# Hybrid attention and HGRN2 block: keys and inputs of three row tiles turned on VectorE and ScalarE instead of TensorE

## What is computed

```python
def hgrn2_chunkwise(q, f_logit, i, lb):
    f = lb[None, None] + (1.0 - lb[None, None]) * jax.nn.sigmoid(f_logit.astype(f32))
    kk = 1.0 - f
    ...
    G = jnp.cumsum(log_f.reshape(B, nc, CHUNK, HGRN_HEADS, HGRN_HEAD_K), axis=2)
    q_dec = qf * jnp.exp(G)
    k_dec = kf * jnp.exp(-G)
    A = jnp.einsum('bclhk,bcmhk->bchlm', q_dec, k_dec)
    A = jnp.where(causal[None, None, None], A, 0.0)
    o_intra = jnp.einsum('bchlm,bcmhv->bclhv', A, vf)
    U = jnp.einsum('bclhk,bclhv->bchkv', k_to_end, vf)
    ...
    o_inter = jnp.einsum('bclhk,bchkv->bclhv', q_dec, S_prev)
```

## Time and profile before

| | us |
|---|---|
| median of 3 executions (890.5 to 892.84) | 891.44 |
| the profiled execution | 892.7 |
| its span, first to last instruction | 890.9 |
| PE busy (4730 matmuls) | 879.2 |
| DVE busy | 524.4 |
| ACT busy | 422.5 |
| POOL busy | 113.9 |

### The profile page before, as it was taken

How to read it: one execution, slowest core, us unless ns; L and a number is a source line. 1 busy time by engine, 2 the same in 40 slices (tenths; PEclk the granted TensorE clock), 3 DMA queues, 4 the chain that set the end, 5 groups by cost and what they waited for, 6 DMA issues and landing times.

```text
span 890.9 us, 12324 instructions
## 1 busy us (share of the span) xinstructions
PE 879.2 (99%) x4730; PEld 721.8 (81%) x4730; DVE 524.4 (59%) x848; ACT 422.5 (47%) x736; POOL 113.9 (13%) x90
## 2 busy tenths in 40 slices
PE   7999999999999999999999999999999999999997
PEld 6887788888888778888888877888888877788886
DVE  6778867864656765665153686465524367655523
ACT  7666456664544444545144534454523453445322
POOL 0000013420200001421020000142111000013012
PEclk9999999999999999999999999999999999999999
DMA  8686766629958543552785654345378544443463
GB/s 313 209 308 221 252 219 226 222 93 376 417 198 303 200 169 132 176 179 98 289 325 197 225 190 142 142 142 194 134 263 330 189 149 158 164 142 144 145 248 127
DMA packets 52922, 186.03 MB, mean 209 GB/s; under 512 B 5888, under 2 KB 6144, under 8 KB 52864
## 3 DMA queue, kind: packets, MB, share of 16 engines
q1 hardware_dynamic: 50128, 178.29, 56.1%
q10 hardware_dynamic: 2736, 6.95, 2.0%
HBM read 141.18 MB, written 44.04 MB: 208 GB/s over the span
## 4 chain that ended last, share of the span: by engine, by line
PE 98%; DMA 1%; issue 0%; DVE 0%; ACT 0%; SPq 0%; DVEq 0%
PE bank L452 65%; PE bank L461 10%; PE score_b L461 5%; PE turn_b L461 5%; PE score_b L481 2%; PE bank L532 2%; PE turn_b L503 2%; PE turn_b L549 2%; PE bank L540 2%; PE turn_b L552 2%; PE score_b L525 1%; PE turn_b L495 1%; DMA x_in<-in_x 1%; PE score_b L559 0%; PE score_b L560 0%; PE turn_b L445 0%
## 5 line engine op out<-in xcount | busy, mean ns | idle before, releaser
L452 PE MATMUL bank<-h_hi,w_hi 128*128 128x512 f32 x832 | 327.4, 395 | 1.6 <-ACT h_hi L728 1.6
L452 PE MATMUL bank<-h_hi,w_lo 128*128 128x512 f32 x832 | 328.0, 394 | 0.0
L452 PE MATMUL bank<-h_lo,w_hi 128*128 128x512 f32 x832 | 325.9, 392 | 0.0
L452 PEld LDWEIGHTS bank<-h_lo,w_hi 128*128 128x128 f32 x832 | 156.5, 188 | 35.1 <-issue 3.3
L452 PEld LDWEIGHTS bank<-h_hi,w_hi 128*128 128x128 f32 x832 | 156.7, 188 | 34.5 <-ACT h_hi L728 1.8
L452 PEld LDWEIGHTS bank<-h_hi,w_lo 128*128 128x128 f32 x832 | 156.7, 188 | 33.7 <-issue 1.0
L1220 POOL TENSOR_TENSOR mix_lo<-v_r,mix_hi 128x512 fp32r<-128x512 f32 x16 | 21.1, 1317 | 544.6 <-ACT v_r L839 544.6
L908 DVE TENSOR_TENSOR w_lo<-w_raw,w_hi 128x1024 fp32r<-128x1024 f32 x37 | 44.9, 1221 | 32.4 <-ACT w_hi L691 32.4
L812 ACT ACTIVATE kv_tok<-score_b 128x1024 f32<-128x1024 f32 x16 | 16.4, 1025 | 83.5 <-PE score_b L525 83.5
L461 PE MATMUL bank<-w_hi,mix_lo 128*128 128x512 f32 x128 | 50.5, 395 | 0.0
L691 ACT ACTIVATE w_hi<-w_raw 128x1024 fp32r<-128x1024 f32 x38 | 39.7, 1051 | 22.1 <-issue 9.3
(11 more groups left out here) (169 smaller groups left out, 1393.8 us busy)
## 6 DMA issues: line engine op xcount, KB each, us to landing
w_hi<-kept_hi SPq DMA_DIRECT2D x96, 512.0 KB, 3.8
w_lo<-kept_lo SPq DMA_DIRECT2D x96, 512.0 KB, 4.7
w_raw<-in_weights SPq DMA_DIRECT2D x38, 512.0 KB, 5.4
kept_hi<-w_hi SPq DMA_DIRECT2D x34, 512.0 KB, 6.0
kept_lo<-w_lo SPq DMA_DIRECT2D x34, 512.0 KB, 7.2
x_in<-in_x_rows SPq DMA_DIRECT2D x8, 1024.0 KB, 7.4
x_in<-in_x SPq DMA_DIRECT2D x15, 512.0 KB, 6.6
out<-q_gate ACTq DMA_DIRECT2D x9, 512.0 KB, 9.0
```

Of the source, the lines that this page charges most:

```text
L452: mm = pe.matmul(acc(w)[:, :], stationary[:, s, k, :], moving[:, k, :], start=(m == 0), stop=(m == 3 * KT - 1), skip_group_check=True)
```

## The change

For tiles 1 to 3 (`DVE_TURN = 1`) PE no longer turns keys and inputs.

- Keys: DVE turns `k_mid` into `kv_tok` by 16 transposes, each of a square of 32 partitions by 32 columns in all four row blocks at once (`turn_keys`, 32x4x32). For heads 1 to 3 they follow the head's `v_r` and `to_next`; for head 0 they stand at the end of that step, behind the softmax of the attention.
- Inputs: DVE turns the 32 by 32 squares of `v_r` in place into `f_d` by one 128x512 transpose. ACT carries the squares to their partitions by 16 copies of 32x4x32 (`place_values`), at the end of its part of the step, behind the two squares of the output of the head before.
- Inputs of heads 1 and 3 go to the upper half of `probs` (`v_spare`), of heads 0 and 2 to `kv_tok` as before.
- `head_sum`, which writes `score_b`, gets the waits on the softmax and on the head before that stood ahead of the transposes. Two waits of PE on `kv_ready` for the use of `score_b` go.

```diff
+DVE_TURN = 1
...
+        def v_tok(t, h):
+            return v_spare if t >= DVE_TURN and h % 2 else kv_tok[:, 1, :]
...
+            def turn_head(t, h):
+
                 pe.wait_ge(m_sub.sem, m_sub.after(t, PAIRS - 1 if gate(h) >= SCORES0 + CHUNKS else (gate(h) - SCORES0) // 2))
                 pe.wait_ge(o_rstd.sem, o_rstd.after(t, h - 2))
                 for a, src in enumerate((k_mid, v_r)):
...
+            def head_scores(t, h):
+
+                pe.wait_ge(k_mid_done.sem, k_mid_done.after(t, h))
+                pe.wait_ge(tile_read.sem, tile_read.after(t, value(h)))
+                if t < DVE_TURN:
+                    turn_head(t, h)
...
                 pe.wait_ge(kv_ready.sem, kv_ready.after(t, h))
+                if t >= DVE_TURN:
+                    pe.wait_ge(k_blocks, blocks_done(t, h))
                 pe.wait_ge(a_masked.sem, a_masked.after(t, h))
...
                 pe.wait_ge(o_low.sem, o_low.after(t, h))
+                if t >= DVE_TURN:
+                    pe.wait_ge(m_sub.sem, m_sub.after(t, PAIRS - 1))
+                    pe.wait_ge(o_rstd.sem, o_rstd.after(t, h - 1))
...
+            def place_values(t, h):
+                act.wait_ge(v_blocks, blocks_done(t, h))
+                act.wait_ge(o_done.sem, o_done.after(t, h - 2))
+                for i in range(4):
+                    for j in range(4):
+                        copy = act.activation(square(v_tok(t, h), j, i), square(f_d[:, :], i, j), ACT.Copy)
+                copy.then_inc(kv_ready.sem, 1)
...
-                        if s == gate(head):
+                        if s == gate(head) and t < DVE_TURN:
                             act.wait_ge(kv_turned.sem, kv_turned.after(t, head))
...
                         if s == out_step(head):
+                            if t >= DVE_TURN and head < HEADS - 1:
+                                act.wait_ge(v_blocks, blocks_done(t, head + 1))
                             act.wait_ge(o_done.sem, o_done.after(t, head))
...
+                    for head in range(HEADS):
+                        if s == gate(head) and t >= DVE_TURN:
+                            place_values(t, head)
...
+            def turn_keys(t, h):
+
+                dve.wait_ge(k_mid_done.sem, k_mid_done.after(t, h))
+                dve.wait_ge(u_done.sem, u_done.after(t, h - 1))
+                for i in range(4):
+                    for j in range(4):
+                        last = dve.transpose(square(kv_tok[:, 0, :], j, i), square(k_mid[:, :], i, j))
+                last.then_inc(k_blocks, 1)
...
+                        if t >= DVE_TURN:
+                            dve.wait_ge(tile_read.sem, tile_read.after(t, value(h_of)))
+                            dve.transpose(f_d[:, :], v_r[:, :]).then_inc(v_blocks, 1)
                         then(t, dve.tensor_tensor(to_next[:, :], to_end[:, h_of % 2, 0:PAIRS - 1], to_mid[:, h_of % 2, 1:], ALU.mult))
+                        if t >= DVE_TURN and h_of:
+                            turn_keys(t, h_of)
...
+                    if s == gate(0) and t >= DVE_TURN:
+                        turn_keys(t, 0)
```

More of the change, by code:

```diff
@@ L180, in hybrid_block @@
         kv_tok = sb("kv_tok", [2, N])
+        v_spare = probs[:, PAIRS:, :].rearrange("p q n -> p (q n)")
         a_t = sb("a_t", [N])
@@ L277, in hybrid_block @@
         y_scaled, finished_pool = count("y_scaled", 2), count("finished_pool", 2)
+        k_blocks, v_blocks = sem("k_blocks"), sem("v_blocks")
         pool_setup = sem("pool_setup")
@@ L312, in wait_split, with blocks_done, square @@
                 engine.wait_ge(w_ready[slot], 32 * uses(slot, FRESH, i + 1))
+        def v_tok(t, h):
+            return v_spare if t >= DVE_TURN and h % 2 else kv_tok[:, 1, :]
+        def blocks_done(t, h):
+            return (t - DVE_TURN) * HEADS + h + 1
+        def square(ap, i, j):
+            return by_pair(ap)[32 * i:32 * i + 32, :, 32 * j:32 * j + 32]
         def state_pairs(t):
@@ L474, in scores @@
                 for h in range(HEADS):
-                    if gate(h) + 1 == SCORES0 + 2 * q:
+                    if gate(h) + 1 == SCORES0 + 2 * q and t < DVE_TURN:
                         pe.wait_ge(kv_ready.sem, kv_ready.after(t, h))
@@ L513, in turn_values @@
                 mm.then_inc(values_turned.sem, 1)
-            def head_scores(t, h):
-                pe.wait_ge(k_mid_done.sem, k_mid_done.after(t, h))
-                pe.wait_ge(tile_read.sem, tile_read.after(t, value(h)))
+            def turn_head(t, h):
                 pe.wait_ge(m_sub.sem, m_sub.after(t, PAIRS - 1 if gate(h) >= SCORES0 + CHUNKS else (gate(h) - SCORES0) // 2))
@@ L537, in head_states @@
                 pe.wait_ge(kv_ready.sem, kv_ready.after(t, h))
+                if t >= DVE_TURN:
+                    pe.wait_ge(k_blocks, blocks_done(t, h))
                 pe.wait_ge(a_masked.sem, a_masked.after(t, h))
                 for p in range(state_pairs(t)):
-                    mm = pe.matmul(head_b[:, pair(p)], kv_tok[:, 0, pair(p)], kv_tok[:, 1, pair(p)], start=True, stop=True)
+                    mm = pe.matmul(head_b[:, pair(p)], kv_tok[:, 0, pair(p)], v_tok(t, h)[:, pair(p)], start=True, stop=True)
                 mm.then_inc(u_done.sem, 1)
@@ L548, in head_out @@
                     empty = t == 0 and p == 0
-                    mm = pe.matmul(out_b[:, pair(p)], kv_tok[:, 1, pair(p)], a_t[:, pair(p)],
+                    mm = pe.matmul(out_b[:, pair(p)], v_tok(t, h)[:, pair(p)], a_t[:, pair(p)],
                                    start=True, stop=empty, skip_group_check=True)
@@ L630, in _ @@
                 pe.wait_ge(mixa_lo.sem, mixa_lo.after(t, QT - 1))
-                pe.wait_ge(kv_ready.sem, kv_ready.after(t, HEADS - 1))
+                if t < DVE_TURN:
+                    pe.wait_ge(kv_ready.sem, kv_ready.after(t, HEADS - 1))
                 order = [(2 * w + i, b) for w in range(3) for b in range(4) for i in range(2)] + [(KT - 2, b) for b in range(4)]
```

## The result

| | before | after |
|---|---|---|
| median, us | 892.14 (4 executions) | 882.98 (4 executions) |
| span of the profiled execution | 890.9 | 882.8 |
| DVE busy | 524.4 | 587.1 |
| ACT busy | 422.5 | 467.5 |

The ratio is 0.9896, interval 0.9884 to 0.9908: 9 us faster. The forecast was 883.6 within 881.8 to 892.0. For the profiled execution it was 884.9, which took 884.64 (892.7 before), 8.1 us less. The medians lie 9.2 apart, partly because a fourth execution of the kernel before moved its median from 891.44, on which the forecast stood, to 892.14.

The account below looks back on a forecast made before the run. PE was taken as the bound, busy 879.2 of 890.9 us. Saving 8.8 us less 1.0 of new waits gave -7.8, 892.7 to 884.9 for the profiled execution; the median, 1.3 lower, was forecast at 883.6, range 881.8 to 892.0.

Parts of the forecast that it names:

- PE's saving: Transposes leaving PE in tiles 1 to 3: 0.74 us saved a head, twelve heads, 8.8 us in all.
- ACT's copies: ACT's 16 copies of turned inputs a head: 0.29 us each from start to start, up to 0.31 allowed, 4.6 us.
- The rope rows: Profile rows of four ACT rope copies of 32x512, 2.40 us together, from which the 0.29 us copy price was taken.
- Rival 1: No new wait: ACT's small copies overlap like full ones (0.19 us), or a chain has more room; 882.6 us, chance 0.22.
- DVE's squares: DVE's 16 transposes of keys a head: 0.30 us each, 4.8 us in all.
- Rivals 2 and 3: Rival 2, and a dearer case: DVE squares at 0.48 us make the mask the bound, 895.3 us, chance 0.16.
- The new wait: PE waits at `A` for head 3's `v_r` in tiles 1 and 2: 0.4 to 0.8 us each, taken as 1.0 together.
- The sum: Whole profiled execution: -8.8 us saved plus 1.0 of waits gives -7.8 us, 892.7 to 884.9.
- Rival 2: DVE squares of about 0.43 us make PE wait for mask and `v_r`, 6.3 us in three tiles; 888.9 us, chance 0.20.
- The turn of the sign at about 0.45: Price of one DVE square, about 0.45 us, from which the change was predicted to make the kernel slower.

Follow-up runs that it names:

- values24: Changed kernel plus 8 more ACT copies a head into a scratch tile that nothing reads; median 895.22 us.
- copies_first: Changed kernel with ACT's 16 copies issued ahead of the two squares of the output of the head before, everywhere; median 883.84 us.
- mixed: Changed kernel with ACT's copies ahead of the output's squares only in heads 1 and 2 of tiles 1 and 2; median 881.52 us.
- keys24: Changed kernel plus 8 more DVE squares of keys a head into a scratch tile that nothing reads; median 889.99 us.

## Why the prediction was right, step by step

- **PE's saving.** Put at 0.74 us a head, 8.8 in all. It is 0.84, as the first product of `A` behind the transposes was 0.1 us slower too: 10.0 in all, 0.1 less in each of the two heads where PE waits, since behind a wait that product is slow as well.
- **ACT's copies.** Put at 0.29 to 0.31, from copies of part height; 0.319 measured. The reason was half right: not the part height but the change of partitions from one copy to the next goes with the missing overlap, as the pairs of values24 show. The rope rows had both. Rival 1 falls, since all 16 copies change partitions. The Trainium skill (ScalarE: Activation LUTs, What ACT_TABLE_LOAD costs) says that instructions in a row overlap by about 93 ns. This case's traces agree for the pairs of values24 (0.31 - 0.22) and nearly for full height (0.12), and disagree for the 16 copies, which leave 12 ns between them.
- **DVE's squares.** Put at 0.30, 0.316 measured; 16 were put at 4.8 us and took 5.05. The prediction's estimate by the Trainium skill (VectorE: DVE Perf Modes, The three transpose paths), 5.0 us, came nearer, though the page's 311 ns is for bf16. Rivals 2 and 3 needed 0.43 and 0.48 and did not come.
- **The new wait.** Forecast at the right place and in the right two tiles, 0.4 to 0.8 us each, taken as 0.5; measured 0.76 and 0.77. The upper end was near because copies cost 0.319 and not 0.29, 0.46 us more for 16; the wait came out 0.36 above the 0.4 that the prediction worked out with 0.29. That ACT holds it is seen in the trace, where the gate's Abs starts the moment ACT is free, and shown by copies_first and mixed, which change only ACT's order, start the Abs 0.8 us earlier and lose the wait.
- **The sum.** 10.0 - 0.2 - 1.5 = 8.3 us against 8.2 in the stretch. The prediction's 7.8 had a saving that was 1.2 too small and a wait that was 0.5 too small; the two errors partly cancel.
- **Rivals 2 and 3.** Their mechanism is real: keys24, at 0.41 a square in effect, has the waits for the mask and for `v_r`. Rival 2 priced 0.43 at 6.3 us of waits and was too low, as keys24 has 8.4, nearly half of it at the two places that the prediction did not name. The turn of the sign at about 0.45 fits: the squares of keys24 are 0.097 dearer each and cost 6.7 us, so the gain of 8.2 is used up at 0.316 + 0.097 x 8.2 / 6.7 = 0.44. This is an estimate that takes the cost as proportional.

## What to carry to other kernels

When PE is the bound and never waits, work can be moved to idle engines at the price of PE's time, but read the room at each place: the span's average said ACT had half its time free, but the copies ended only 1.4 us ahead of PE's product in heads 1 and 2 of tile 1 and 1.1 in head 3, and the gate chain behind them had no room at all. Move small transposes as a whole group, because much of what they cost is the switch in and out. Before moving a step on one engine, ask what the next engine down the chain does with it: a copy moved on ACT moved POOL's low parts onto DVE's path. When you price a row of short instructions, look whether neighbours start at the same partitions; and when you add instructions to make a step dearer, measure how much dearer it became.

## What the runs showed of the hardware

- Sixteen transposes of 64 partitions cost PE 0.49 us and 0.35 us of switching: 0.1 us ahead of them, 0.15 behind, and 0.1 in the first 128-partition matmul that follows.
- fp32 transposes on DVE: 303 ns for 32x128 and 711 ns for 128x512.
- In these traces DVE and ACT start an instruction of part height before the one ahead has ended only where both start at the same partitions. 32-partition copies on ACT: 0.22 us from start to start in the pairs of values24, 0.319 where the partitions change. 32-partition transposes on DVE: 0.24 in the pairs of keys24, 0.316 where they change. The first copy of heads 1 to 3, which starts at partition 0 like the full-height square ahead, begins 0.12 us before that one ends.
- DVE's transposes are not held by POOL: 16 take 5.05 us at 369.36, while POOL runs for 2.5 us of it, and 5.05 at 315.29, where POOL is idle. DVE instructions that start during one of POOL's are held until it ends in these rows: a subtraction of two SBUF tensors (1.73 us for 0.69), a copy (1.07 for 0.17) and a scaling (1.31 for 0.28).
